# Attention's output projections, the norm and the router of a mixture-of-experts layer, put into one block

## The reference, cut to what matters

```python
merged = sigmoid(hn @ w_gs) * y_ssm + sigmoid(hn @ w_ga) * (o_nsa @ w_nsa_out)
h = h + gate1 * (merged @ w_o)
hn2 = _rmsnorm(h, norm2_g) * (1.0 + scale2) + shift2
# _hier_moe(hn2): 4 groups x 8 experts; softmax over groups, best group; softmax over its
# experts, best two; every expert e: (silu(t @ w_g[e]) * (t @ w_u[e])) @ w_d[e], weighted
h = h + gate2 * _hier_moe(hn2, ...)
return _rmsnorm(h, final_g)
```

## Time and profile before

| | us |
|---|---|
| median of 3 runs | 3182.69 |
| the profiled execution, its own time | 3186.31 |
| its span (first to last instruction) | 3184.1 |
| TensorE busy, matmuls | 2894.7 (91%) |
| VectorE busy | 1528.4 (48%) |
| ScalarE busy | 1007.5 (32%) |
| GpSimd busy | 321.7 (10%) |

### The profile page before, as it was taken

The page is one execution under the profiler, slowest core; times in us unless marked ns, Lnnn a source line. Parts: engine busy times, 40 slices in busy tenths (PEclk is TensorE's granted clock), DMA queues, the critical chain, the costliest instruction groups (busy, mean ns, idle before and its releaser), DMA issues. The chain is left out here.

```text
span 3184.1 us, 35108 instructions
## 1 busy us (share of the span) xinstructions
PE 2894.7 (91%) x14335; PEld 2290.3 (72%) x14335; DVE 1528.4 (48%) x2008; ACT 1007.5 (32%) x1411; POOL 321.7 (10%) x203
## 2 busy tenths in 40 slices
PE   6899999999989999999979899999779896699994
PEld 5777788888777778888858788877556575577772
DVE  4652355555465235455556356564658734111113
ACT  3244432223225343222223233352128722111111
POOL 0000003444000001244400000010000000100001
PEclk8999999999999999999989899999879896799996
DMA  4221143444221113334422233332422012599992
GB/s 121 70 63 40 56 130 109 131 133 132 73 67 53 46 60 126 116 116 132 132 65 86 73 100 96 100 123 79 143 79 103 2 53 81 201 368 368 367 329 111
DMA packets 280359, 384.80 MB, mean 121 GB/s; under 512 B 53636, under 2 KB 250500, under 8 KB 267140
## 3 DMA queue, kind: packets, MB, share of 16 engines
q1 hardware_dynamic: 269348, 344.74, 33.0%
q0 software_dynamic: 10752, 37.75, 3.1%
q10 hardware_dynamic: 96, 0.02, 0.0%
HBM read 340.50 MB, written 41.94 MB: 120 GB/s over the span
## 5 line engine op out<-in xcount | busy, mean ns | idle before, releaser
L195 PE MATMUL ps<-h_hi,w_hi 128*128 128x512 f32 x1760 | 712.7, 405 | 58.4 <-DVE room L814 19.2
L196 PE MATMUL ps<-h_lo,w_hi 128*128 128x512 f32 x1760 | 699.8, 398 | 0.0
L197 PE MATMUL ps<-h_hi,w_lo 128*128 128x512 f32 x1760 | 698.9, 397 | 0.0
L172 ACT ACTIVATE w_hi<-w_raw 128x2048 fp32r<-128x2048 f32 (+1 forms) x170 | 322.2, 1896 | 891.5 <-PE ps L197 883.3
L177 DVE TENSOR_TENSOR w_lo<-w_raw,w_hi 128x2048 fp32r<-128x2048 f32 (+1 forms) x170 | 431.3, 2537 | 255.2 <-ACT w_hi L172 255.2
L195 PEld LDWEIGHTS ps<-h_hi,w_hi 128*128 128x128 f32 x1760 | 337.6, 192 | 145.9 <-issue 70.9
L197 PEld LDWEIGHTS ps<-h_hi,w_lo 128*128 128x128 f32 x1760 | 336.7, 191 | 74.6
L196 PEld LDWEIGHTS ps<-h_lo,w_hi 128*128 128x128 f32 x1760 | 337.8, 192 | 73.0 <-issue 2.4
L196 PE MATMUL ps<-merged_lo,w_hi 128*128 128x512 f32 x640 | 255.4, 399 | 0.0
L195 PE MATMUL ps<-merged_hi,w_hi 128*128 128x512 f32 x640 | 252.2, 394 | 0.0
L197 PE MATMUL ps<-merged_hi,w_lo 128*128 128x512 f32 x640 | 250.9, 392 | 0.0
(11 more groups left out here) (418 smaller groups left out, 4071.4 us busy)
## 6 DMA issues: line engine op xcount, KB each, us to landing
w_raw<-in_w_in SPq DMA_DIRECT2D x284, 256.0 KB, 3.7
w_raw<-in_w_up SPq DMA_DIRECT2D x128, 256.0 KB, 3.5
w_raw<-in_w_down SPq DMA_DIRECT2D x128, 256.0 KB, 3.6
w_more<-in_w_exp_down SPq DMA_DIRECT2D x32, 1024.0 KB, 7.8
room<-in_w_ada SPq DMA_DIRECT2D x96, 256.0 KB, 6.0
w_raw<-in_w_exp_gate SPq DMA_DIRECT2D x16, 1024.0 KB, 9.0
w_raw<-in_w_exp_up SPq DMA_DIRECT2D x16, 1024.0 KB, 7.3
w_more<-in_w_exp_gate SPq DMA_DIRECT2D x16, 1024.0 KB, 9.4
```

The lines of the kernel that those rows point to most:

```text
L172: act.activation(self.hi[:, q, :, 0:cols], raw[:, q, :, 0:cols], ACT.Copy).then_inc(self.hi_ready, 1)
L195: pe.matmul(out, w[0], x[0], start=start, stop=False)
L196: pe.matmul(out, w[0], x[1], start=False, stop=False)
L197: return pe.matmul(out, w[1], x[0], start=False, stop=stop)
```

## The change

The stages `nsa_out`, `w_o` and `route` become one, `nsa_end`. In it:

- The norm is not applied to `x` before the router. With g2 the norm's gain (scale included), rs the token's reciprocal root and s the shift, the router's input is `x*g2*rs + s`. The kernel splits `x*g2` for each chunk as soon as that chunk of `x` is there, makes logits and turned rows from it, and multiplies the results by rs for each token afterwards; the bias gets `s @ w` added (`bias_ps`), the rows get `s` (`shift`, a broadcast made by TensorE).
- `w_o` signals after each chunk (`half`, `column`) and its first tile goes through the contraction chunk by chunk (`m_low`). Logits of chunks 0 to 3 and turns of chunks 0 and 1 stand between the columns of the last two `w_o` tiles; turns 2 and 3 and all of chunks 4 to 7 come behind the last column.
- The sum of squares is made per token with matmuls of 1 column (`sums`), so root and reciprocal work on [128, 4] in place of [128, 512].
- ScalarE's order has fewer `keep` operations between the two exponentials, and the tables are loaded ahead.
- The scatter waits per token block for `rows_ready`.
- Only expert 0's weights are loaded in this stage; expert 1's go into `w_second`, which takes the room of the split `merged`, and are issued in `moe` behind the rows of experts 0 and 1. The buffers of `moe` and `combine` move into room that is already there. `rest_rows` (norm for the conditional part) is new, under the condition.

The diff's core:

```diff
-            self.nsa_out()
-            self.add_projection("w_o", B2 + P_WO, self.m, ..., scale=lambda k: self.p2("ada", 2 * KC + k, 1), last=True)
-            self.route()
+                    self.nsa_end()
+                self.w_second = sbuf(until_moe, "expert_second", [P, 3, KC * COL])
             @block.sync
+                for name, at, count in (("w_router_group_2", 0, MG), ("w_router_expert_2", MG, NE)):
+                    sp.dma_start(raw[:, :, at:at + count], ...).then_inc(landed, 16)
+                self.issue2(sp, P_NSAO, P_MOE)
+                self.issue_expert(sp, 0, 2)
+                for i in range(2):
+                    sp.wait_ge(W.lo_ready, 2 * (WO + 1) + i + 1)
+                    self.issue_expert(sp, 0, i)
             @block.tensor
+                def vectors():
+                    pe.wait_ge(landed, 32)
+                    for k in range(KC):
+                        mm = pe.matmul(bias_ps, shift_of(k).to_broadcast([P, P]), raw[:, k, :], start=k == 0, stop=k == KC - 1)
+                    mm.then_inc(bias_ready, 1)
+                    for k in range(KC):
+                        mm = pe.matmul(self.ps[:, 6 + k // 4, ...], shift_of(k).to_broadcast([P, P]), self.c("ident"), start=True, stop=True)
+                    mm.then_inc(shift_ready, 1)
+                def logits(k):
+                    pe.wait_ge(x_low, k + 1)
+                    for t in range(TB):
+                        for x, w in ((h_hi, hi), (h_hi, lo), (h_lo, hi)):
+                            mm = pe.matmul(lg_ps[:, t, :], x[:, k, toks(t)], w[:, k, :], ...)
+                def turn(k):
+                    pe.wait_ge(x_low, k + 1)
+                    if k >= 2:
+                        pe.wait_ge(kept, k - 1)
...
+                def sums(squares, first, at):
+                    for t in range(TB):
+                        for c in at:
+                            mm = pe.matmul(sum_ps[:, t:t + 1], squares[:, c, toks(t)], self.c("ones")[:, 0:1], ...)
+                for t, (m, q) in enumerate(nsa):
+                    tile_columns(pe, W, m, q, self.pst, self.h)
+                    if t == 1:
+                        vectors()
+                m, q = wo[0]
+                W.ready(pe, m, q)
+                for k in range(KC):
+                    if k % n == 0:
+                        pe.wait_ge(m_low, k // n + 1)
...
+                for t in range(1, 4):
+                    column(t, 0)
+                    if t >= 2:
+                        logits(2 * t - 4)
+                        logits(2 * t - 3)
+                    column(t, 1)
+                    if t >= 2:
+                        turn(2 * t - 4)
+                        turn(2 * t - 3)
+                pe.wait_ge(biased, 1)
+                pe.wait_ge(sq_added, 2)
+                sums(acc, True, range(n))
+                logits(4)
+                logits(5)
+                logits(6)
+                pe.wait_ge(last_sq, 2)
+                sums(last, False, range(n)).then_inc(summed, 1)
+                logits(7)
+                for k in range(4, KC):
+                    turn(k)
             @block.scalar
+                act.preload_act_table_set(SQRT)
+                for t, (m, q) in enumerate(wo):
+                    if t < 2:
+                        W.split_hi(act, m + 1, q)
+                    for c in range(n):
...
+                        act.activation(h_hi[:, k, :], self.x[:, k, :], ACT.Copy, scale=self.p2("g2", k, 1)).then_inc(x_hi, 1)
+                    if t < 3:
+                        act.activation(acc if t == 0 else more, pair(self.x, t), ACT.Square).then_inc(x_sq, 1)
+                    if t >= 2:
+                        keep(2 * t - 4)
+                        keep(2 * t - 3)
+                act.wait_ge(mean, 1)
+                act.activation(self.rs_tok[:], self.rs_tok[:], ACT.Sqrt).then_inc(root, 1)
+                act.preload_act_table_set(EXP_LN)
+                act.wait_ge(shifted, 1)
+                act.activation(eg[:], eg[:], ACT.Exp).then_inc(expd, 1)
+                keep(4)
+                keep(5)
+                act.wait_ge(shifted, 2)
+                act.activation(e8[:], e8[:], ACT.Exp).then_inc(expd, 1)
+                keep(6)
+                keep(7)
             @block.vector
+                for t, (m, q) in enumerate(wo):
+                    for c in range(n):
...
+                        dve.scalar_tensor_tensor(self.x[:, k, :], self.pst[:, q, c], ..., ALU.mult, ALU.add)
+                        if t == 3:
+                            dve.tensor_tensor(last[:, c], self.x[:, k, :], self.x[:, k, :], ALU.mult).then_inc(last_sq, 1)
+                        dve.wait_ge(x_hi, k + 1)
+                        dve.scalar_tensor_tensor(h_lo[:, k, :], self.x[:, k, :], self.p2("g2", k, 1), h_hi[:, k, :].bitcast(F32), ALU.mult, ALU.subtract).then_inc(x_low, 1)
+                    if t < 2:
+                        W.split_lo(dve, m + 1, q)
+                    if t in (1, 2):
+                        dve.wait_ge(x_sq, t + 1)
+                        dve.tensor_tensor(acc, acc, more, ALU.add).then_inc(sq_added, 1)
+                dve.wait_ge(summed, 1)
+                dve.tensor_scalar(self.rs_tok[:], sum_ps, 1.0 / D, EPS, ALU.mult, ALU.add).then_inc(mean, 1)
+                dve.wait_ge(root, 1)
+                dve.reciprocal(self.rs_tok[:], self.rs_tok[:]).then_inc(rs_ready, 1)
+                dve.wait_ge(logits_done, 1)
+                for t in range(TB):
+                    e = dve.scalar_tensor_tensor(lg[:, t], lg_ps[:, t], self.rs_tok[:, t:t + 1], bias[:], ALU.mult, ALU.add)
+                def rows(t):
+                    dve.scalar_tensor_tensor(self.h_tok[:, t, :], self.h_tok[:, t, :], self.rs_tok[:, t:t + 1], shift..., ALU.mult, ALU.add).then_inc(rows_ready, 1)
                     e.then_inc(chosen, 1)
+                dve.wait_ge(kept, KC)
+                for t in range(TB - 1):
+                    rows(t)
                 dve.wait_ge(counted, 1)
...
+                rows(TB - 1)
             @block.gpsimd
                 pool.wait_ge(placed, 2)
-                pool.wait_ge(kept, KC)
                 for t in range(TB):
+                    pool.wait_ge(rows_ready, t + 1)
 def moe(self):
             @block.sync
-                for e in range(XR):
+                for e in range(2):
+                    rows_of(e)
+                for i in range(3):
+                    self.issue_expert(sp, 1, i)
+                for e in range(2, XR):
                     rows_of(e)
```

More of the change, by code:

```diff
@@ L24 @@
 EXP_LN = "natural_log_exp_and_others"
+SQRT = "sqrt_and_others"
 NEG = -1e30
@@ L2598, in route @@
[L2598 to L2606 removed]
+            sem, clear = self.stages.open("nsa_end", st)
@@ L2618, in route @@
             block = st.enter_context(nc.Block())
+            pair = lambda a, t: a[:, n * t:n * t + n, :]
+            acc, more, shift, last = (pair(self.merged, t) for t in range(4))
+            h_hi, h_lo = self.h
+            toks = lambda t: slice(t * P, (t + 1) * P)
+            shift_of = lambda k: self.p2("ada", 3 * KC + k, 1)
+            lg_ps = self.ps[:, 2, 0:TB * NR].rearrange("p (t r) -> p t r", t=TB)
+            bias_ps, sum_ps = self.ps[:, 3, 0:NR], self.ps[:, 3, 0:TB]
+            turn_ps = lambda k: self.ps[:, 6 + k % 2, :]
```

355 lines of the change are left out of this document (187 added, 168 removed).

## The result

The changed kernel takes 3143.88 us (median of 4 runs, 3143.62 to 3145.84), the kernel before on the same chip 3184.2 (4 runs, 3181.23 to 3186.5). The ratio is 0.9875, 95% interval 0.9858 to 0.9892. The forecast was 3139.4, with a range from 3130 to 3149. The profiled execution of the changed kernel spans 3142.2 us (before 3184.1) at a mean granted clock of 0.946 (0.936): 41.9 us between the spans.

What follows compares the result with a forecast made beforehand. Stages run serially, with TensorE's gap before `w_o`, the norm, half-clock logits and turns, and VectorE's routing chain on the path. Places at 2683.9 against 2727.15 gain 43.3 us: 3182.7 - 43.3 = 3139.4 us; range 3130 to 3149.

Steps and rivals of the forecast that it cites:

- The new E: End of `w_o`: 2650.2, 1.9 us later than before; the closed gap's 10.2 us are spent on added narrow matmuls.
- The chosen 1.4 us for one fall of the clock: Inside `w_o`, where 24 narrow matmuls stand together: the clock may fall, costing between nothing and 3.0 us; 1.4 taken.
- The work by chunk is hidden: VectorE's per-chunk work in `w_o` takes some 7.7 us with waits, under a tile of 11.2 us, so costs nothing.
- From E to the places: From `w_o`'s end to the routing places: 33.7 us, places at 2683.9 against 2727.15, with a chain of 17.2 us.
- Its three terms: VectorE's routing chain of 27.1 us: less 2.9 (first exponential), less 7.4 (second exponential), plus 0.4 (four bias operations).
- the 2.9 us of the first exponential: Routing chain: VectorE's wait for the first exponential falls from 3.2 to 0.3 us, as its table is loaded.
- Rows in the count's wait: Routing chain: three `rows` operations of 1.28 us each and 0.5 for weights, 4.3 us, hidden in a 4.6 us wait.
- Behind the places: Scatter and start of `moe` keep their 14.6 us; the moved weight loads are hidden with 3 us to spare.
- Rival 1: The clock holds through the tail behind `w_o` and in `w_o`: 7.0 us less, 3132.4 us; chance 0.25.
- rival 2: Half clock from `w_o`'s end on, full clock price inside `w_o`: 6.0 us more, 3145.4 us; chance 0.12.
- Rival 3: The gap before `w_o` isn't closed, or VectorE's per-chunk work holds TensorE up: 3149 us; chance 0.08.
- Rival 4: Slower: expert 1's 3 MB or new buffers make every `moe` load late; 3201 at 2 us an expert; chance 0.03.

Runs made afterwards that it cites:

- the second experiment: Against the changed kernel, ScalarE's tail order put back: no early exponential table load, all four last row-tile copies ahead of the second exponential; 3149.45 us.
- the gap's kernel: Against the changed kernel, TensorE waits for all four multiplications by the sigmoids (`m_low` 4) before `w_o`'s first tile, so the stages no longer overlap; 3153.18 us.

## Why the prediction was right, point by point

**The new E.** Forecast 1.9 us later than before, measured 2.0 (74.43 - 72.41). Its terms hold one by one. `vectors` takes 2569.53 to 2573.01, where the next wide matmul starts: 3.5 us, forecast 3.6. From `nsa_out`'s last tile to E it is 2648.75 - 2595.28 = 53.5 us, forecast 4 x 11.2 + 7.2 + 1.4 = 53.4. The chosen 1.4 us for one fall of the clock, between 0 and 3.0 without a row that said where, was 1.5 to 1.7: the window at 0.50 is 3.4 us long and does half its work, and moving the second group away gives 1.5 beyond its matmuls.

**The work by chunk is hidden.** VectorE has the next tile's low part at 2611.97 + 2.29 = 2614.26, 8.5 us after the tile before was done; the forecast said 7.7 of 11.2. No matmul in `w_o` waits.

**From E to the places.** The sums come at E + 13.95, forecast 13.7. The clock falls after 4.0 us, forecast 4.7 from the one stretch that showed such a fall. The logits are read at E + 16.96, forecast 16.5: 0.3 us more for the sums, 0.2 between the last sums and the last logits. The chain then takes 2682.90 - 2665.71 = 17.2 us, forecast 17.2. Its three terms are right in size. One reason was only partly right: the 2.9 us of the first exponential were put down to its table being loaded ahead. The load is 1.28 of them; the other 1.6 are the `keep` ahead of it and the wait for its turn, and the second experiment shows that without a `keep` in between the load comes early by itself.

That the tail came within 0.3 us is partly luck. The same narrow tail lost the clock 4.0 us behind E here and 2.9 in the gap's kernel, where the places then came 1.0 us later; the forecast had one row for this time, of another shape of matmul.

**Rows in the count's wait.** 3.67 us of rows and 0.49 of weights, and 0.57 us of waiting left: hidden as forecast.

**Behind the places** 2.4 us were lost that the forecast had at nothing, in three terms. First, places to the row loads takes 15.4 us, not 14.6: the first scatter lasts 1.86 us and not 1.09. From the start of the `CAST` it is 14.80 before and 15.55 to 15.59 in all eleven kernels with the change (to SyncE's first issue), so this belongs to the change; why the first scatter lasts longer was not tried. Second, from the first row load to the first weighted product it is 17.6 us, before 17.2: the clock comes back 12.4 us behind the row loads instead of 11.4. Third, in `combine` the third gather's second half lands 2.58 us late in this execution:

```profile
3098.12 1.28 DVE L3041 SCALAR_TENSOR_TENSOR nsa_gate<-token_out,place_weight,nsa_gate 128x1024 f32<-128x1024 f32 x1 [2.58 <-DMA token_out<-slot_out,place]
```

From the last gather's issue to the update of `x` it takes 9.5 us here, 7.9 before, and 7.5 to 9.5 in the experiments, so that is scatter between executions. Against that, the final stage was 0.6 us shorter.

**Against the medians.** Forecast -43.3; the traces give -42.7 by the places and +2.4 behind them, -40.3, which is also the difference of the medians. The time forecast, 3139.4, was missed by 4.5 us: 0.6 by the places, 2.4 behind them, and 1.5 because the kernel before has a median of 3184.2 beside the changed kernel and not the 3182.7 that the forecast started from. So the median lies inside the whole range, but 0.9 us outside the forecast's own one of 3135 to 3143.

**Rivals.** Rival 1 (the clock holds) and rival 2 (half from E on) bracket the result. The median alone is nearer to rival 2 (3145.4) than to the forecast; it is the windows that decide against both: full clock for 4.0 us behind E, and the fall inside `w_o` at about half of its full price. Rival 3 (the gap or VectorE's pace) would have shown as a bracket at 2595.08. Rival 4 (late weight loads) has its measure now: gate weights landed in 8.9 us against 9.4 before, and 3 MB put in the wrong place cost 8 us once, not 2 us an expert.

**The rule weighed.** In the changed kernel the granted clock falls to 0.50, 1.2 GHz, in a stretch where TensorE is busy for 4.00 of 4.00 us, and in the experiment with wide matmuls among the narrow ones it stays there for 18.1 us, with TensorE busy for all of them. The rule of the Trainium skill, page "TensorE: Matmul & The Clock Gate", section "HAM oscillation — how this bites in real kernels", by which idle gaps cost the clock, agrees with the first experiment (5.91 us idle, clock lost in it) and not with these two windows. What exactly the chip counts stays open: nine wide logits in a row, behind the same turns and sums, went with a clock that stayed, 22 wide ones scattered among narrow ones didn't keep it.

## What to carry to other kernels

Fold a per-token factor into what is read last, logits and rows, instead of into the operand, when the factor needs a reduction over everything; that took the norm out of the path and was, with ScalarE's order, worth most (some 25 of 40 us). Then look which operand is stationary: a matmul of 36 columns on a stationary tile of 128 took 0.112 us at full clock, about as long as one of 128 or of 1, and turning it round saved 11.5 us, more than the overlap by chunk (8.9). When work is moved from a bound engine's full stretch to a tail, count what the tail's other engines still have to do; the last two microseconds moved came back as a wait for copies.

## What was not expected of the hardware

A narrow matmul's price follows TensorE's clock: 0.112 us at 1.0, 24.90 / 117 = 0.213 at 0.50, and the recorded time of its weight load goes from a mean of 191 to 330 ns:

```profile
L2577 PEld LDWEIGHTS ps<-route_hi,h_hi 128*128 128x128 f32 x8 | 1.5, 191 | 0.0
```

```profile
L2577 PEld LDWEIGHTS ps<-route_hi,h_hi 128*128 128x128 f32 x10 | 3.3, 330 | 0.0
```

The first is at full clock (2638.5 to 2642), the second at half (2652.7 to 2661). With 36 stationary columns a load is recorded with 113 ns. The Trainium skill, page "TensorE: Matmul & The Clock Gate", section "LDWEIGHTS (loading the stationary operand)", gives the load as the stationary columns divided by 1.2 GHz, by estimate 107 ns for 128 and 30 for 36. The spacing of 0.112 us here at full clock is near the first, and 0.213 at half isn't; the section has no other figure for it. The recorded loads, 191 and 113 ns, are longer than either estimate.

The table for the exponential is loaded 0.02 to 0.03 us behind the square root whether or not the program asks for it early, ahead of the wait that stands before the exponential (2663.12 in the changed kernel, 2668.05 in the second experiment). In the kernel before, with a `keep` in between, it came directly behind that `keep`.
